# Local attention on 160 keys per query half, with the tokens held in grid-column order

## The reference

```python
xn = _rmsnorm(x, norm_pre_w[l])
h = xn @ w_in[l]                      # 2048 x 13312
na_q, na_k, na_v, na_z, hg_q, hg_ff, hg_fb, hg_i, hg_z, gate_pre = jnp.split(h, splits, axis=-1)
# neighbourhood attention, 16 heads of 64: all 4 rows, but only 16 columns around the query
cs = jnp.clip(qc - NA_WIN_COLS // 2, 0, GRID_W - NA_WIN_COLS)
col_mask = (kc[None, :] >= cs[:, None]) & (kc[None, :] < cs[:, None] + NA_WIN_COLS)
s = jnp.einsum('bqhd,bjkhd->bhqjk', qr, kb) * scale + bias   # bias by (row, column) distance
s = jnp.where(col_mask[None, None, :, None, :], s, -jnp.inf)
p = jax.nn.softmax(s.reshape(B, H, GRID_W, wr * GRID_W), axis=-1)
o_a = jnp.einsum('bhqn,bnhd->bqhd', p, vb) * jax.nn.silu(na_z)
# the second branch: a gated linear recurrence over the tokens in row order, both directions
o_b = _rmsnorm(_hgrn2_bidirectional(...)) * jax.nn.silu(hg_z)
y = g_a * (o_a @ w_branch[l, :NA_WIDTH]) + g_b * (o_b @ w_branch[l, NA_WIDTH:])
x = x + _rmsnorm(y @ w_out[l], norm_post_w[l])
```

## Time and profile before

| what | us |
|---|---|
| median of 3 runs | 826.64 (826.08 to 828.06) |
| the profiled execution, its own device time | 826.77 |
| its span, first to last instruction | 824.8 |
| TensorE busy | 814.3 (99%) |
| VectorE busy | 629.4 (76%) |
| ScalarE busy | 408.4 (50%) |
| GpSimd busy | 40.8 (5%) |
| mean granted TensorE clock | 0.998 |

### The profile page before, as it was taken

One profiled execution on the slowest core, in us unless ns is written; L12 is line 12 of the kernel. 1 busy time (PEld: TensorE's weight loads), 2 busy tenths in 40 slices (PEclk: granted clock), 3 DMA queues, 4 the chain that ended last, 5 costly groups with the idle time before them and its releaser, 6 DMA issues.

```text
span 824.8 us, 13692 instructions
## 1 busy us (share of the span) xinstructions
PE 814.3 (99%) x5582; PEld 704.2 (85%) x5582; DVE 629.4 (76%) x1053; ACT 408.4 (50%) x690; POOL 40.8 (5%) x48
## 2 busy tenths in 40 slices
PE   9999999999999999999999999999999999999996
PEld 7888888888888888888888888888888888888884
DVE  4776757888888888888888888888784788875543
ACT  5745535445445445445445445445454555544442
POOL 4000100000000000000000000000000000000002
PEclk9999999999999999999999999999999999999999
DMA  9756867676576576576676576675575866676522
GB/s 331 276 164 201 212 186 180 176 201 169 163 201 167 164 200 166 165 201 163 168 201 171 161 199 165 170 195 155 162 197 160 235 177 195 204 265 230 183 87 102
DMA packets 246733, 154.01 MB, mean 187 GB/s; under 512 B 15288, under 2 KB 228368, under 8 KB 246288
## 3 DMA queue, kind: packets, MB, share of 16 engines
q1 hardware_dynamic: 245664, 149.17, 63.8%
q10 hardware_dynamic: 1008, 3.98, 1.3%
HBM read 151.04 MB, written 2.10 MB: 186 GB/s over the span
## 4 chain that ended last, share of the span: by engine, by line
PE 97%; DMA 1%; DVE 0%; ACT 0%; POOL 0%; POOLq 0%; issue 0%; ACTq 0%
PE psum L1150 46%; PE psum L1158 24%; PE psum L1209 3%; PE psum L1393 3%; PE psum L1395 3%; PE psum L1210 3%; PE psum L1211 3%; PE psum L1394 3%; PE psum L1262 1%; PE psum L1250 1%; PE psum L1225 1%; PE psum L1295 1%; PE psum L1238 1%; PE psum L1285 1%; DMA big<-in_x 1%; PE psum L1173 0%
## 5 line engine op out<-in xcount | busy, mean ns | idle before, releaser
L691 DVE TENSOR_TENSOR w_lo<-raw,w_hi 128x1024 fp32r<-128x1024 f32 x272 | 321.8, 1220 | 77.1 <-ACT w_hi L437 77.0
L1150 PE MATMUL psum<-act_hl,w_hi 128*128 128x512 f32 x1408 | 335.9, 391 | 0.0
L1150 PEld LDWEIGHTS psum<-act_hl,w_hi 128*128 128x128 f32 x1408 | 258.8, 188 | 50.1
L437 ACT ACTIVATE w_hi<-raw 128x1024 fp32r<-128x1024 f32 x272 | 273.5, 1053 | 39.0 <-PE psum L1395 27.2
L1158 PE MATMUL psum<-act_hl,w_lo 128*128 128x256 f32 x1408 | 186.2, 285 | 0.0
L1158 PEld LDWEIGHTS psum<-act_hl,w_lo 128*128 128x128 f32 x1408 | 177.4, 191 | 4.1
L451 ACT ACTIVATE part<-psum 128x256 f32<-128x256 f32 x88 | 33.5, 380 | 180.3 <-PE psum L1158 180.3
L1150 PE MATMUL psum<-branch_hl,w_hi 128*128 128x512 f32 x256 | 61.4, 391 | 0.7 <-DVE branch_hl L899 0.7
L1150 PEld LDWEIGHTS psum<-branch_hl,w_hi 128*128 128x128 f32 x256 | 46.9, 188 | 10.2 <-issue 1.1
L1209 PE MATMUL psum<-w_hi,branch_hl 128*128 128x512 f32 x128 | 50.2, 392 | 0.3 <-DVE branch_hl L982 0.3
L1393 PE MATMUL psum<-w_hi,act_hl 128*128 128x512 f32 x128 | 49.9, 390 | 0.0
(11 more groups left out here) (135 smaller groups left out, 677.6 us busy)
## 6 DMA issues: line engine op xcount, KB each, us to landing
raw<-in_w_in SPq DMA_DIRECT2D x103, 1024.0 KB, 5.8
raw<-in_w_branch SPq DMA_DIRECT2D x16, 1024.0 KB, 6.0
raw<-in_w_out SPq DMA_DIRECT2D x16, 1024.0 KB, 5.1
bias_t<-in_na_rel_bias SPq DMA_DIRECT2D x32, 96.0 KB, 5.9
big<-in_x SPq DMA_DIRECT2D x4, 512.0 KB, 8.6
big<-in_x ACTq DMA_DIRECT2D x2, 1024.0 KB, 6.0
out<-big SPq DMA_DIRECT2D x5, 256.0 KB, 2.4
raw<-in_w_in SPq DMA_DIRECT2D x2, 512.0 KB, 6.8
```

Of the source, the lines that this page charges most:

```text
L437: nc.scalar.activation(w_hi[:, (2 * r + h) % HALVES, :], raw[:, r, 1024 * h:1024 * (h + 1)], ACT.Copy).then_inc(hi_ready, 1)
L691: nc.vector.tensor_tensor(w_lo[:, i, :], raw[:, r, 1024 * h:1024 * (h + 1)], w_hi[:, i, :].bitcast(F32), ALU.subtract).then_inc(lo_ready, 1)
L1150: nc.tensor.matmul(sums[h][:, :], w_hi[:, i, w], operand[:, k, :], start=k == 0 if whole else k % 8 == 0, stop=False, skip_group_check=True)
```

## The change

1. **Order of the tokens.** `act_hl` gets its tokens in column order (column, then row): the adding step of `scale_pair` writes with a stride of four elements, and so do the matmuls that spread the per-token factors. Keys, values, queries and SiLU gate of the attention stay in that order (queries and gate within a half by rows, reversed); results for the other branch, and the gates, are brought back to row order as they leave PSUM (`take_tile`), and the attention output as it is split for the branch projection.
2. **Early tiles.** I now comes from tiles 0 to 7, V from tiles 8 to 15, and V is made of `act_hl`, so tile 8 + r, half h waits for pair 2r + h of it. The steps that make `act_hl` are listed by a table (`ACT_HI`, `ACT_LO`) and stand in tiles 5 to 10 instead of 6 to 14.
3. **Scores** of a query half are taken against 160 keys; bias, maximum, exponential and normalisation too. Normalised probabilities go to a tensor `prob_n` of 256 keys per half, whose rest GpSimd clears once.
4. **Turning.** Per head two 128 x 128 transposes, and for the 32 queries of the other half that see a tile of keys, two plain fp32 matmuls of 32 columns with columns of the identity.
5. **Heads' output.** 8 matmuls of 128 columns and 8 of 32 columns instead of 8 of 256.
6. **Bias.** Eight transfers per group (one per head and query row) into `bias_raw`, behind a wait for GpSimd's masks of the group before; GpSimd makes four additions per group into `bias_m`, behind a wait for the scores of the group before. The masks are made in other places of SBUF and set up with more selections; three additions and the clearing of `prob_n` stand behind waits for the factors (`rows_ready`) and the gate set-up.

```diff
+HALF_W = GRID_W // 2
+SPAN = 40
+EDGE = SPAN - HALF_W
+REACH = SPAN + EDGE
+KEYS = ROWS * SPAN
...
+ACT_HI = {6: (0, 1), 7: (2, 3), 8: (4,), 9: (5, 6), 10: (7,)}
+ACT_LO = {5: (("scale", 0), ("scale", 1)), 6: (("lo", 0), ("lo", 1), ("scale", 2)),
...
             def load_bias(g):
-                wait(sp, s_taken, g * 2)
-                for parity in range(2):
+                wait(sp, bias_ready, g * 4)
+                for rq in range(ROWS):
                     for a in range(2):
...
-                col = (V_TILE if c < 2 else I_TILE) * P + (c % 2) * 512
+                col = (I_TILE if c < 2 else V_TILE) * P + (c % 2) * 512
...
+            pool.wait_ge(rows_ready, 1)
+            pool.wait_ge(vec_ready, 2)
+            for r in range(1, ROWS):
+                nc.gpsimd.tensor_tensor(win[:, :, :], win_parts[:, :, 0, :] if r == 1 else win[:, :, :],
+                                        win_parts[:, :, r, :], ALU.add).then_inc(win_ready, 1)
+                pool.wait_ge(win_ready, r)
+            nc.gpsimd.memset(prob_n[:, :, :, :], 0.0).then_inc(prob_clear, 1)
+
             def mask_bias(g):
-                pool.wait_ge(bias_landed, g * 64 + 64)
-                v = bias_t[:, :, :].rearrange("p a (m c) -> p (a m) c", c=GRID_W)
-                w = win[:, 0:1, :].to_broadcast([P, 12, GRID_W])
-                nc.gpsimd.tensor_tensor(v, v, w, ALU.add).then_inc(bias_ready, 1)
+                pool.wait_ge(bias_landed, g * 128 + 128)
+                wait(pool, s_taken, g * 2)
+                for u in range(2):
+                    w = win[:, u:u + 1, :].to_broadcast([P, ROWS, SPAN])
+                    for a in range(2):
+                        v = bias_raw[:, a * ROWS:(a + 1) * ROWS, EDGE * (1 - u):EDGE * (1 - u) + SPAN]
+                        nc.gpsimd.tensor_tensor(by_columns(bias_m[:, u, a, :]), v, w, ALU.add).then_inc(bias_ready, 1)
...
+                src, prt = ps_proj[b][:, 0:T], part[:, b, :]
+                if dst is na_q or dst is na_z:
+                    dst = by_queries(dst)
+                    src = src.rearrange("p (u c r) -> p u r c", u=2, r=ROWS)
+                    prt = prt.rearrange("p (u c r) -> p u r c", u=2, r=ROWS)
+                elif dst is not na_k:
+                    dst, src, prt = by_rows(dst), by_columns(src), by_columns(prt)
...
-                nc.vector.tensor_tensor(v, x_hl[:, 2 * i:2 * i + 2, 0:T].bitcast(F32),
-                                        x_hl[:, 2 * i:2 * i + 2, T:2 * T].bitcast(F32), ALU.add).then_inc(xs_step, 1)
+                pair = x_hl[:, 2 * i:2 * i + 2, :].bitcast(F32)
+                wait(dve, act_ready, i - 1)
+                nc.vector.tensor_tensor(v.rearrange("p k (c r) -> p k r c", r=ROWS),
+                                        pair[:, :, 0:T].rearrange("p k (r c) -> p k r c", r=ROWS),
+                                        pair[:, :, T:2 * T].rearrange("p k (r c) -> p k r c", r=ROWS),
+                                        ALU.add).then_inc(xs_step, 1)
...
+                    if c == 2:
+                        pe.wait_ge(act_ready, 2 * r + h + 1)
...
-                            ins = nc.tensor.matmul(ps_heads[a][:, u * T:(u + 1) * T], left[rows, q], right[rows, k],
-                                                   start=(i == 0), stop=(i == 2))
+                            ins = nc.tensor.matmul(ps_heads[a][:, u * T:u * T + KEYS], left[rows, q],
+                                                   keys_of(right[rows, k], u), start=(i == 0), stop=(i == 2))
...
                 for kt in range(2):
-                    for t in range(2):
-                        u = 1 - t
-                        ins = nc.tensor.transpose(ps_pt[:, kt * T + t * P:kt * T + (t + 1) * P],
-                                                  prob[:, a, u * T + kt * P:u * T + (kt + 1) * P], block[:, 0, :])
+                    for u in (kt, 1 - kt):
+                        block_of = prob_n[:, a, u, kt * P:(kt + 1) * P]
+                        if u == kt:
+                            ins = nc.tensor.transpose(ps_pt[:, kt * T:kt * T + P], block_of, block[:, 0, :])
+                        else:
+                            ins = nc.tensor.matmul(ps_pt[:, kt * T + P:kt * T + P + ROWS * EDGE], block_of,
+                                                   edge_of(block[:, 0, :], kt), start=True, stop=True)
...
-                for kt in range(2):
-                    for c in range(0, P, STRIP):
-                        ins = nc.tensor.matmul(ps_o[c:c + STRIP, 0:T], v_now[:, kt * P + c:kt * P + c + STRIP],
-                                               prob_t[:, c // HEAD, kt * T:(kt + 1) * T], start=(kt == 0), stop=(kt == 1))
+                for edge in range(2):
+                    for kt in range(2):
+                        for c in range(0, P, STRIP):
+                            seen = prob_t[:, c // HEAD, kt * T:(kt + 1) * T]
+                            if edge:
+                                dst = edge_of(ps_o[c:c + STRIP, (1 - kt) * P:(2 - kt) * P], kt)
+                                seen = seen[:, P:P + ROWS * EDGE].rearrange("p (r c) -> p r c", c=EDGE)
+                            else:
+                                dst, seen = ps_o[c:c + STRIP, kt * P:(kt + 1) * P], seen[:, 0:P]
+                            ins = nc.tensor.matmul(dst, v_now[:, kt * P + c:kt * P + c + STRIP], seen,
+                                                   start=(edge + kt == 0), stop=(edge == 1), skip_group_check=True)
```

139 lines of the change are left out of this document (82 added, 57 removed).

## The result

The changed kernel takes 828.75 us, the median of ten runs (827.70 to 829.68); ten runs of the kernel before beside it have a median of 826.66 (826.08 to 828.06). The ratio is 1.0025 by these medians; the comparison gives 1.002 with a 95% interval of 1.0013 to 1.0028. The change costs a quarter of a per cent, about 2 us, which is inside the 0.3% called "same". The forecast was 827.3, with a range of 824.5 to 836.0; the interval does not reach a ratio of 1, so the 2 us are clear of the noise; 0.6 of them were forecast.

What follows compares the result with a forecast made beforehand. TensorE, busy 99% of the span, was taken as the bound. Scores -0.3, turning +2.6, heads' output -2.2 and early-tile stall +0.5 gave +0.6 us, so 827.3 us; range 824.5 to 836.0, the forecast's own range 825.5 to 829.5.

Steps and rivals of the forecast that it cites:

- The pace of small matmuls: TensorE: under 256 moving fp32r columns, or 128 plain fp32, a full-width stationary load sets the pace; fewer columns win nothing.
- Scores: Score matmuls at 160 columns: step stays 117 ns, only the last pair ends sooner; -0.04 us per group, -0.3 in all.
- Turning: Transposing the probabilities: two transposes and four product records per head, 601 ns against 436; +2.6 us for sixteen heads.
- The rule: TensorE: distance of two matmul starts is the longer of the moving time and the next weight load's time.
- Heads' output: Heads' output matmuls: 32-wide stationary operands, so loads do not count; 0.62 against 0.89 us per group, -2.2 us.
- Early tiles: Tiles 8 to 11: TensorE waits for VectorE's pairs, 1.5 us to spare; stall put at 0.5 us, bounds 0 and 4.
- The upper bound: Early-tile stall of 4 us, if each strided adding step on VectorE doubled: 8 x 0.69 - 1.5.
- The second suspect: Early tiles: GpSimd clearing 1024 elements beside VectorE may slow it and eat of the 1.5 us to spare.
- What else moves: VectorE, GpSimd, SyncE and ScalarE work in the groups, strided results at most 0.15 us more each; all costed at nothing.
- narrow fp32r products: Rival, scores: 160-column fp32r runs like plain fp32, 275 ns per pair instead of 117; +7.6 us, 835.2 us, chance 0.25.
- only the columns counting: Rival, groups: loads do not set the pace, so scores, turning and output all win; -5.5, 821.1 us, chance 0.13.
- Late pairs: Rival, early tiles: strided writes and clearing exceed the 1.5 us to spare; up to +3.5 on the forecast, 830.8 us, chance 0.07.

Runs made afterwards that it cites:

- scores256: Changed kernel with score products of 256 key columns instead of 160, scores of the second tile not right; one execution, 829.24 us.
- four_turns: Changed kernel with four transposes per head again instead of two transposes and two 32-column products; median 824.59 us, ratio 0.9967 to the kernel before.
- clear_first: Changed kernel with GpSimd's clearing of prob_n moved to the start of its work, strided write kept; median 828.63 us.
- plain_write: Changed kernel with the adding step writing its 512 elements side by side instead of every fourth; median 827.04 us, ratio 1.0009 to the kernel before.
- x_by_sync: Changed kernel with the two late loads of x issued by SyncE instead of ScalarE; median 827.94 us, ratio 1.0009 to the kernel before.

## Why the prediction came out as it did

**The pace of small matmuls.** Right for the time of a row of matmuls, and tested at three widths and in two orders: with 128 stationary columns the mean step does not fall under 109 to 110 ns, however few columns move. The Trainium skill, "TensorE: Matmul & The Clock Gate", section "LDWEIGHTS (loading the stationary operand)", gives the load as the stationary columns divided by 1.2, in ns, whatever the rows; for 128 columns that makes 107 ns, an estimate from the page's formula. The step of 110 ns between the 64-row loads of the scores agrees.

**Scores.** Forecast -0.04 us per group, measured -0.08 by the slot and -0.07 by the starts. The step was taken to stay at 117 ns, read from the earlier trace rows and put down to the load; but at 256 columns it is the columns that give 116 to 117, and below them the load gives 110. The mis-sized term is -0.3, which measured -0.6 (8 x 0.07); scores256 shows the 6.67 us of before again, so the width alone makes it.

**Turning.** +2.6 forecast, 16 x 0.18 = +2.9 measured; four_turns took the same 2.9 back out. The rule holds for the sum, not for each distance. From the first transpose (139.19) to the next run (139.72) the rows of after show 0.53 us in steps of 0.11, 0.14, 0.14 and 0.14, where the rule has 0.11 from a transpose to a product and 0.17 or 0.22 from a product to what follows. The run of 16 behind takes 2.00 us where a plain one takes 1.91. So the turning costs 0.53 + 0.09 = 0.62, against 0.36 + 0.08 = 0.44 before.

**Heads' output.** -2.2 forecast, 8 x 0.29 = -2.3 measured.

**Early tiles.** Right in place (first half of tile 11) and in what is waited for (the seventh lo part of a pair), wrong in size: 0.5 forecast, 1.4 measured. The failed step is the cost of the strided write, +0.15 us per addition from L788, where it is +0.40. L788 writes in order and alternates between two places in one source; it was near in size, not in kind. The upper bound, each strided step doubled, would have given 4; with the measured 1.09 the forecast's own sum gives 1.7. The second suspect, GpSimd's clearing, cost at most some hundredths of a us (clear_first). The Trainium skill, "SBUF — State Buffer", section "Door 1", gives four fp32 elements as the distance up to which a stride is free, and in the same note a penalty for each access that goes to a new line of 16 bytes, which is what this stride does. The distance is not free here: 1088 ns against 686 for the same addition. The measurement decides; with no price for the stride the stall would have been zero, as in plain_write.

**What else moves.** The work on VectorE in the groups held no one up, as said. `take_tile` with strides cost 615 ns instead of 425, 0.19 us instead of the 0.15 at most, without effect. The late issue of x had no term in the sum; moving it to SyncE is worth 0.8 to 1.0 us in the changed kernel (x_by_sync) and 0.3 in the one before, so it adds about 0.6 to the difference of the two. Why the changed kernel pays more is open.

**The sum.** By the measured terms -0.6 + 2.9 - 2.3 + 1.4 = +1.4 from the change, where +0.6 was forecast, and about 0.6 from the issue of x: from the 826.7 of the kernel before that makes 828.7, and 828.8 was measured. In the groups the forecast had some luck: its errors there (-0.3, +0.3 and -0.1) cancel. In the stall and in the issue of x it had none, and it was 1.4 us too low. That the wide range holds the result says little, since it reached up to 836.0 for narrow fp32r products; the forecast's own range, 825.5 to 829.5, holds it as well. Two of the rivals did not occur: with only the columns counting the turning slot would have been 5.90; with narrow fp32r products at the price of plain fp32 the scores slot would have been 7.6. Late pairs is what occurred, at 1.4 us instead of the 3.5 + 0.5 of that rival, so it stayed within the forecast's own range.

## What to carry to other kernels

Before cutting the moving columns of small matmuls, set their time beside the next weight load: below it a cut wins next to nothing, and splitting one product into more adds a full load for each. Where a change gives a non-bounding engine dearer work, sum that engine's work up to the moment at which the bounding engine wants the result; 1.5 us to spare is little when one access pattern adds 0.4 us eight times. And look at DMA issues on an engine whose next instruction is on that path: the same two issues held it for 0.83 us in some profiles and for up to 2.03 in others.

## What the runs showed of the hardware

- VectorE, an addition of 512 fp32 elements per partition in SBUF: 0.69 us in order, 1.09 us written at every fourth element, 1.28 us with both sources read at every 64th.
- fp32r matmuls with 128 stationary columns are not dearer per product at 160 or at 64 moving columns than at 256: a pair of the scores takes 110 ns at both, 116 at 256.
- The turning of one head: four transposes 0.44 us, two transposes and two 32-column plain fp32 products in turns 0.62 us, the same with both transposes first 0.67 us.
- Issuing two 1 MB loads held ScalarE for 0.83 us in five profiles and for up to 2.03 in six others, with the same code; from SyncE it took 0.81 or 0.82 in three profiles.
